# Moving an output projection into the stage behind it, with its norm taken from sums and four tiles in front

## The reference, cut to what matters

```python
# first block, its end
y = concat([ssd_out_norm(...), gdn_out_norm(...)])          # 512 x 2048
merge = rms_norm(y @ w_out, post_w)
h_lat = h_lat + gate_l * merge       # gate_l: a third of silu(c) @ w_ada + b_ada
# second block, twice
h = rmsnorm(x, norm_g[l])
proj = h @ w_in[l]                   # conv, q, k, v, gates, memory queries
...                                  # convolution, attention with two softmaxes per head, memory attention
x = x + concat([y_a, y_d, y_m]) @ w_out[l]
```

## Time and profile before

| | |
|---|---|
| median of 3 runs | 3633.96 us (3632.18 to 3634.73) |
| the profiled execution, its own time | 3634.55 us |
| its span | 3632.8 us |
| TensorE, VectorE, ScalarE, GpSimd busy | 95%, 47%, 41%, 9% of the span |
| mixing stage's products | about 235 to 1058 us |
| output projection's products | 1551.0 to 1740.0 us |
| first product of layer 0, of layer 1 | 1797.1 us, 2715.9 us |

### The profile page before, as it was taken

How to read it: one execution, slowest core, us unless ns; L and a number is a source line. 1 busy time by engine, 2 the same in 40 slices (tenths; PEclk the granted TensorE clock), 3 DMA queues, 4 the chain that set the end, 5 groups by cost and what they waited for, 6 DMA issues and landing times.

```text
span 3632.8 us, 53291 instructions
## 1 busy us (share of the span) xinstructions
PE 3439.6 (95%) x21996; PEld 2811.6 (77%) x21996; DVE 1712.8 (47%) x2813; ACT 1480.5 (41%) x2296; POOL 318.0 (9%) x334
## 2 busy tenths in 40 slices
PE   7999999999978989799699999999999999999998
PEld 5888888888857878678377777887777777788787
DVE  7665564565525656544744444333234444443422
ACT  6564443344325353232365555222225555632211
POOL 0000230130003323100200000000100000000000
PEclk9999999999989999899799999999999999999999
DMA  9642332333440010165322222333432222233342
GB/s 375 209 143 61 91 101 71 86 105 102 126 163 25 15 49 26 46 212 203 136 87 75 81 83 85 103 99 99 145 104 81 81 81 81 76 104 96 96 139 81
DMA packets 150081, 383.39 MB, mean 106 GB/s; under 512 B 14257, under 2 KB 39089, under 8 KB 149841
## 3 DMA queue, kind: packets, MB, share of 16 engines
q1 hardware_dynamic: 138384, 338.44, 29.5%
q0 software_dynamic: 11456, 41.56, 3.3%
HBM read 350.38 MB, written 29.56 MB: 105 GB/s over the span
## 4 chain that ended last, share of the span: by engine, by line
PE 49%; DVE 1%; ACT 0%; issue 0%; DVEq 0%; POOL 0%; ACTq 0%
PE lay_acc L2478 42%; PE lay_nb L2494 1%; PE lay_sA L2533 1%; PE lay_ob L2551 1%; PE lay_om L2478 1%; PE lay_tb L2512 1%; DVE lay_four L2895 1%; DVE lay_u_lo L2899 0%; PE lay_om L2561 0%; DVE lay_wlo L2774 0%; DVE lay_u_lo L2904 0%; ACT lay_whi L2615 0%; PE lay_tb L2518 0%; PE lay_sA L2541 0%; PE lay_sB L2541 0%
## 5 line engine op out<-in xcount | busy, mean ns | idle before, releaser
L2478 PE MATMUL lay_acc<-lay_u_hi,lay_whi 128*128 128x512 f32 x2240 | 898.7, 401 | 0.0
L2478 PE MATMUL lay_acc<-lay_u_hi,lay_wlo 128*128 128x512 f32 x2240 | 875.4, 391 | 0.0
L2478 PE MATMUL lay_acc<-lay_u_lo,lay_whi 128*128 128x512 f32 x2240 | 874.2, 390 | 0.0
L2774 DVE TENSOR_TENSOR lay_wlo<-lay_stage,lay_whi 128x1024 fp32r<-128x1024 f32 x288 | 360.9, 1255 | 528.6 <-ACT lay_whi L2615 527.9
L2478 PEld LDWEIGHTS lay_acc<-lay_u_hi,lay_whi 128*128 128x128 f32 x2240 | 422.0, 188 | 106.9 <-issue 21.9
L2615 ACT ACTIVATE lay_whi<-lay_stage 128x1024 fp32r<-128x1024 f32 x288 | 303.0, 1054 | 477.1 <-PE lay_acc L2478 417.1
L2478 PEld LDWEIGHTS lay_acc<-lay_u_lo,lay_whi 128*128 128x128 f32 x2240 | 422.2, 188 | 91.1 <-issue 6.7
L2478 PEld LDWEIGHTS lay_acc<-lay_u_hi,lay_wlo 128*128 128x128 f32 x2240 | 421.6, 188 | 89.9
L842 PE MATMUL proj_lat<-proj_u_hi,proj_whi 128*128 128x512 f32 x832 | 339.2, 408 | 8.2 <-DVE proj_wlo L1058 8.2
L842 PE MATMUL proj_lat<-proj_u_hi,proj_wlo 128*128 128x512 f32 x832 | 327.0, 393 | 0.0
L842 PE MATMUL proj_lat<-proj_u_lo,proj_whi 128*128 128x512 f32 x832 | 326.4, 392 | 0.0
(11 more groups left out here) (413 smaller groups left out, 5459.5 us busy)
## 6 DMA issues: line engine op xcount, KB each, us to landing
lay_stage<-units_dram SPq DMA_DIRECT2D x288, 512.0 KB, 3.6
tokens_unit_stage<-in_units_dram SPq DMA_DIRECT2D x212, 256.0 KB, 2.7
front_stage<-in_w_ada_dram SPq DMA_DIRECT2D x64, 512.0 KB, 5.5
front_stage<-in_w_kv_dram SPq DMA_DIRECT2D x32, 512.0 KB, 4.7
out_stage<-in_w_out_dram SPq DMA_DIRECT2D x16, 1024.0 KB, 5.6
out_wg<-in_w_ada_dram POOLq DMA_DIRECT2D x32, 512.0 KB, 4.8
tokens_x_sb<-scr_arow SPq DMA_DIRECT2D x32, 256.0 KB, 4.5
tokens_x_sb<-in_xT_dram SPq DMA_DIRECT2D x4, 1536.0 KB, 10.4
```

The lines of the kernel that those rows point to most:

```text
L2478: mm = pe.matmul(bank_of(t)[:], w[:, i % SLOTS, k, :], u[:, kt, :], start=(kt == n == 0), stop=(kt == KT - 1 and n == 2))
L2774: dve.tensor_tensor(wlo[:, i % SLOTS, :, :], stage[:, i % DEEP, :, :], whi[:, i % SLOTS, :, :].bitcast(F32), ALU.subtract)\
```

## The change

The output projection is no longer a stage of its own.

- It heads `layers`: 32 units of 512 KB (`out_units`), the first two tiles as a pair, four PSUM banks in turn. y is loaded into x's place in six parts (`Y_PARTS`); x is loaded into the same place once the low parts of y have been left (`y_left`), on SyncE's queue ahead of the fifth unit.
- The gate's 64 operations go to the mixing stage (`add_gate` there, one a unit, outside the stretches in which the scan's weights are made), with 64 loads of 256 KB and four stores on SyncE's queue. `layers` reads the sums back (1 MB, GpSimd's queue) and turns them on TensorE in unit 5.
- The sum of squares over tiles is made by VectorE (`o_sum`) with two more, of x times the gated result and of the gated result squared, so that the norm of the new x follows from three sums without making x first. Root and reciprocal become Ln and Exp on ScalarE. The scaling moves to VectorE (`add_out`), two tiles ahead of `make_u`.
- Each layer starts with four tiles together instead of two: first half of four, then second half of four (`LEAD_TILES`), tile 3 in the bank `ob`; head 0's side work comes two beats later (`HEAD_AT[0] += 2`). `between` of the four is called behind each half.

```diff
-    def project_out(...)  and class Stream
...
+    gate_load_at = {i + DEEP - 1: q * KT + kt for i, (q, kt) in gate_at.items()}
...
                     if i - 2 in head_at:
                         weights(head_at[i - 2])
+                    if i in gate_at:
+                        add_gate(*gate_at[i])
...
+LEAD_TILES = 4
+UNITS = [(_t, _half) for _half in range(2) for _t in range(LEAD_TILES)]
...
+                for g in range(4):
+                    sp.wait_ge(y_left, 4 * g + 4)
+                    sp.dma_start(x[:, 4 * g:4 * g + 4, :], dr.xT...[:, 4 * g:4 * g + 4, 0:LAT]).then_inc(x_loaded[g], 16)
+                for g in range(NX):
+                    if g + DEEP < NX:
+                        load_out_unit(g + DEEP)
...
                         if UNITS[j][0] in PAIRS and UNITS[j][1] == 0:
-                            for part in (i, i + 2):
-                                start_unit(part)
-                                start_unit(part + 1)
+                            many = LEAD_TILES if j == 0 else 2
+                            for part in (i, i + many):
+                                for n in range(many):
+                                    start_unit(part + n)
                                 for k in range(UK):
-                                    for n in range(2):
+                                    for n in range(many):
                                         mm = products(part + n, k, True)
                                         if k == UK - 1:
                                             mm.then_inc(unit_done, 1)
-                                between(part)
-                                between(part + 1)
-                            j += 4
+                                for n in range(many):
+                                    between(part + n)
+                            j += 2 * many
...
+                take_out(KT - 1)
+                square_gated(KT - 1)
+                act.wait_ge(o_summed, 1)
+                act.activation(o_rs, nb[:], ACT.Ln, bias=eps[:, 1:2], scale=1.0 / D).then_inc(o_logged, 1)
+                act.activation(o_rs, o_rs, ACT.Exp, scale=-0.5).then_inc(o_rs_ready, 1)
+                split(LEAD)
+                act.wait_ge(var_ready, 1)
+                act.activation(x_rs[:], var, ACT.Ln).then_inc(o_logged, 1)
+                act.activation(x_rs[:], x_rs[:], ACT.Exp, scale=-0.5).then_inc(x_rs_ready, 1)
...
+                cross_out(KT - 1)
+                make_var()
+                add_out(0)
+                split(LEAD)
+                add_out(1)
+                dve.wait_ge(x_rs_ready, 1)
+                for k in range(KT + 1):
+                    make_u(0, [k])
+                    if k + 2 < KT:
+                        add_out(k + 2)
+                    if UK + 1 <= k < UK + 1 + LEAD_TILES:
+                        split(LEAD + k - UK)
                 for i in range(NQ_ALL + 1):
...
-                    if i == 0:
-                        make_u(0, range(4 * LEAD, KT + 1))
-                    elif i == NU:
+                    if i == NU:
                         dve.wait_ge(rs_ready, 1)
                         make_u(1, range(KT + 1))
-                    if i + LEAD < NQ_ALL:
+                    if i > LEAD_TILES and i + LEAD < NQ_ALL:
                         split(i + LEAD)
```

More of the change, by code:

```diff
@@ L428, in _ @@
                         take_kv(r)
[L431 to L499, removed]
@@ L607, in project_and_scan @@
     cb_at = {26: 0, last[tile_no["C", 1]] + 8: 1}
+    free = [i for i in range(LEAD * W_U + 2, NU) if not any(HEAD0[g] <= i < HEAD0[g] + 4 * HG for g in range(SSD_G))]
+    gate_at, gate_stored_at = {}, {}
+    for q in range(D // 512):
+        for kt in range(KT):
+            gate_at[free.pop(0)] = (q, kt)
+        gate_stored_at[max(gate_at) + 1 + DEEP] = q
+        free = free[2:]
+    gate_load_at = {i + DEEP - 1: q * KT + kt for i, (q, kt) in gate_at.items()}
     with Phase(nc, "proj") as ph:
@@ L2222 @@
 PAIRS = (0, N_IN)
[L2223 to L2225 removed]
+LEAD_TILES = 4
+UNITS = [(_t, _half) for _half in range(2) for _t in range(LEAD_TILES)]
+for _t in range(LEAD_TILES, len(TILES)):
+    if _t == N_IN:
         UNITS += [(_t, 0), (_t + 1, 0), (_t, 1), (_t + 1, 1)]
[L2227 removed]
+    elif _t != N_IN + 1:
         UNITS += [(_t, 0), (_t, 1)]
@@ L2581, in _ @@
                 pe.wait_ge(c_loaded, 32)
+                for part in (0, 2):
+                    pe.wait_ge(lo_ready, part + 2)
+                    for k in range(UK):
+                        for n in range(2):
+                            mm = out_products(part + n, k, True)
+                            if k == UK - 1:
+                                mm.then_inc(unit_done, 1)
+                for g in range(4, NX):
+                    n, h = O_UNITS[g]
+                    if h == 0 and n >= 4:
+                        pe.wait_ge(o_taken, n - 3)
+                    pe.wait_ge(lo_ready, g + 1)
+                    for k in range(UK):
+                        mm = out_products(g, k, False)
+                    mm.then_inc(unit_done, 1)
+                    if g == TURN_GATE:
+                        turn_gate()
+                out_sums()
                 for l in range(LAYERS):
@@ new lines, in make_gamma, with add_up @@
+                def make_gamma():
+                    dve.wait_ge(g_turned, 1)
+                    b0, w0 = COL["b_ada"] + 2 * KT, COL["post_norm_w"]
+                    dve.tensor_tensor(gam[:], tb[:, 0:KT], cols[:, b0:b0 + KT], ALU.add)
+                    dve.drain()
+                    dve.tensor_tensor(gam[:], gam[:], cols[:, w0:w0 + KT], ALU.mult)
+                    dve.drain().then_inc(gam_ready, 1)
+                def add_up(n, total, part, done):
+                    if n == 0:
+                        dve.tensor_copy(total, part).then_inc(done, 1)
+                    else:
+                        dve.tensor_tensor(total, total, part, ALU.add).then_inc(done, 1)
@@ L2777, in evacuate, with add_out @@
+                def add_out(k):
+                    dve.tensor_tensor(res[:, k, :], res[:, k, :], o_rs, ALU.mult)
+                    dve.drain()
+                    dve.scalar_tensor_tensor(out=x[:, k, :], in0=res[:, k, :], scalar=gam[:, k:k + 1], in1=x[:, k, :], op0=ALU.mult, op1=ALU.add)\
+                        .then_inc(x1_added, 1)
                 def evacuate(l, t):
```

488 lines of the change are left out of this document (257 added, 231 removed).

## The result

The changed kernel takes 3677.65 us (median of four runs, 3672.53 to 3683.07) against 3634.35 of the kernel before: ratio 1.012, 95% interval 1.0103 to 1.0138. It is slower by some 43 us; the forecast was 21 slower, and the time lies 1.7 above the top of the range. The profiled execution is the longest of the four, 3683.07 with a span of 3681.3: 48.5 above the span of the earlier trace rows's execution.

The account below looks back on a forecast made before the run. TensorE, busy 95% of the span, was taken as the bound. 36.8 us lost in layer 1, less 17.4 won up to layer 0's unit 8, plus 2 for mixing gave +21.4 on 3634.55: 3656, range 3637 to 3676.

Parts of the forecast that it names:

- the restart 3.0 and 1.9 of side work: At unit 8 of each layer: TensorE's restart at low clock plus a sum and one block of scores moved later, 4.9 us.
- I take no wait: Fifth unit of the projection: its halves ready at 1571.1, TensorE there at 1571.4, so no wait.
- Start of the projection: Projection's first product: earlier loads let TensorE begin at 1546.7 in place of 1551.03, 4.3 us won.
- the third rival: Projection's fifth unit is late because x's 4 MB stand ahead of it: 8 us more, 3664; chance 0.13.
- The projection: Projection's products: last one ends at 1727.3 in place of 1740.0, 8.4 us won beyond the earlier start.
- The tail: Last product of the projection to layer 0's first: 17.4 us in place of 57.1.
- The lead of layer 0: First four tiles of layer 0: second half starts at 36.5 us after TensorE idles 12, lead ends at 61.2.
- The gaps: Between lead and unit 8: sums and turns wait for ScalarE or VectorE, 21.3 us in layer 0, 19.3 in layer 1.
- the first rival: Ahead of unit 8 in both layers: the gap closes itself, 40.6 us less, 3615; chance 0.10.
- Layer 1: Start of layer 1: first product waits for the fourth unit's low part behind `make_u`; unit 8 comes 36.8 us later.
- The gate in the mixing stage: Mixing stage: the gate's added operations and loads cost 2 us, ends nothing and 20.
- The fourth rival: Mixing stage pays: VectorE's bursts meet the gate's loads, 20 us in place of 2, 3674; chance 0.11.

Follow-up runs that it names:

- x_behind: Changed kernel with units 5 to 8 of the projection loaded ahead of x's four parts on SyncE's queue: 3673.6 us, ratio 1.0099 to the kernel before.
- turn_later: Changed kernel with head 1's v turned one beat later: 3665.1 us, ratio 1.0075 to the kernel before.
- before_again: The kernel before, unaltered, profiled once more: 3636.3 us in one run.
- gate_out: Changed kernel without 56 of the gate's 64 operations and their loads in the mixing stage: 3671.8 us, one run.
- side_later: Changed kernel with head 0's side work four beats later in place of two, memory turns and second memory norm moved: 3645.5 us, ratio 1.0023 to the kernel before.
- gate_loads: Changed kernel with the gate's 64 loads kept, but 56 of its 64 operations replaced by a copy of one column: 3681.7 us, one run.
- gate_later: Changed kernel with the gate's operations beginning at beat 30 of the mixing stage in place of 14: 3677.4 us, ratio 1.0111 to the kernel before.

## Why the prediction was right in direction and short in size

Two steps failed. The first is "the restart 3.0 and 1.9 of side work": it gives 4.9 a layer to what comes behind unit 8, where 11.1 and 12.4 were measured, since two turns on one bank meet at beat 17 and TensorE waits. The second is "I take no wait" at the fifth unit. Either is a wait put at nothing; the large terms, the tail, the lead, the gaps and the start of layer 1, came as written. Term by term:

- *Start of the projection*: -3.6, forecast -4.3. Near, with luck: this execution has 17.5 from the end of gdn to the first product, the other eleven that have the change 14.2 to 17.3, most of them about 15, which would be -6.
- *The fifth unit, "I take no wait"*: failed. The sum left 0.3 us between demand and low part, and the wait was 2.1 to 4.3 in the nine executions that load x first. In the profile TensorE came 23.9 behind its first product (24.7 in the sum), and began the unit at 26.9 (24.4 in the sum): it was the load that was mis-sized. With the low clock behind it 5 to 6 us, and the projection as a whole 6 to 7 (`x_behind`). This is the third rival (8 us), which I gave 0.13.
- *The projection*: 180.9 without that wait, where the steps give 180.6. Near because two errors cancel: in `x_behind` the first four units took 23.6 in place of 24.7, and the gate's turned columns 5.2 in place of 3.8, with low clock behind them, for which the sum has no term.
- *The tail*: 17.3 against 17.4 (the terms as written add up to 17.15). Right. A table load of 1.28 stands between Ln and Exp here too, so the rows were the right guide. ScalarE behind the last product:

```profile
1746.11 1.28 ACT L2679 ACT_TABLE_LOAD   x1
1747.41 0.69 ACT L2679 ACTIVATE lay_room<-lay_nb,lay_eps 128x512 f32<-128x512 f32 x1
1748.11 1.28 ACT L2681 ACT_TABLE_LOAD   x1
```

- *The lead of layer 0*: middle at +36.1 (36.5), end at +60.6 (61.2). Right.
- *The gaps*: 20.9 and 19.3 (21.3 and 19.3). Right; the first rival, that they close, did not happen.
- *Layer 1*: the low part behind `make_u` cost 20.4 of 30.4, shown by moving it alone. Right.
- *"The restart 3.0 and 1.9 of side work"*: the step that failed most. 4.9 a layer was forecast, 11.1 and 12.4 were measured; 6.4 and 6.7 of them are the collision of two turns at beat 17 (`turn_later`). I priced the two beats' shift at the work that it carries past unit 8, and did not lay the shifted table over head 1's. The restart itself cost 2.3 and 2.6 at unit 8, less than the 3.0 that I took.
- *The gate in the mixing stage*: +4.6, forecast +2 with ends 0 and 20. Right in kind: operations on VectorE at a burst, not loads. The fourth rival, 20, did not happen.
- *gdn*: 4.9 of the profiled difference, forecast 0. Not shown to be a part of the change (`before_again`).

So the 27 us by which the profiled difference exceeds the forecast are 13 (turns), 7 (fifth unit), 5 (gdn) and 2.6 (mixing), and what is left, -1, is small terms of both signs. In the medians the excess is 21.7, since the profiled execution is 5.4 longer than the median; which terms are smaller there no trace shows. With the turns' 13 alone the forecast would have been 3669.

## What to carry to other kernels

Work in front of a stage can be taken away in full (40 us here) and be lost again by what leads the next one: when a start asks for more at once, ask which of its inputs stands behind a long row on the engine that makes it, and what small work then has no products over it. When one head's table of beats is shifted, lay it over the next head's and look for two uses of one bank in one place. A transfer that the sum finds in time by only 0.3 us deserves a term of its own: here it was late by 2.1 to 4.3.

## What the runs showed of the hardware

- TensorE's clock can fall some time after a restart. After 2.84 us idle the first product took 0.50 and four took 0.39 to 0.40, the next eight 0.58 to 0.63, at a granted clock of 0.51 with 1.00 before and behind them; that cost 1.7. After 4.04 idle (the middle of layer 1's lead) the low products came at once, 1.7 as well; after 11.8 idle ten intervals took 4.32 in place of 2.26.
- The length of a short idle did not settle what it cost. Over the nine executions with a wait at the fifth unit the unit's 24 products lost 0.1 to 3.0: 0.1 after 2.78 (`gate_out`), 0.2 after 3.48 (`side_later`, where the clock held 1.00), 1.8 after 2.84 and 3.0 after 4.20 (`gate_loads`). In the mixing stage of `gate_later` seven more products ran slowly behind an interval of 2.62, and in the changed kernel none behind one of 2.65. `side_later` at the fifth unit, in one row its longer idle, in the next full speed:

```profile
1582.46 0.50 PE L2359 MATMUL lay_sA<-lay_u_hi,lay_whi 128*128 128x512 f32 x1 [3.48 <-DVE lay_wlo L2739]
1582.79 0.39 PE L2359 MATMUL lay_sA<-lay_u_lo,lay_whi 128*128 128x512 f32 x1
```

- One stage whose code no version changes took 456.7 to 465.9 us from execution to execution. A difference of 5 us in a single pair of profiles can't be given to a change until the same kernel is profiled twice; here one repeat took a tenth of the profiled loss out of the change's account.
